# Expert rows gated on the way out and added by the scatter to residual rows in HBM, in a two-layer encoder with a mixture of experts

## The reference

```python
for i in range(2):
    h = rms_norm(x, norm1_g[i])
    x = x + (conformer_conv(h) if i == 0 else diff_attention(h))
    h = rms_norm(x, norm2_g[i])
    x = x + hierarchical_moe(h)

def hierarchical_moe(h):                 # 512 tokens, 32 experts in 4 groups of 8
    grp_p, grp_idx = top_k(softmax(h @ w_grp + b_grp), 1)
    top_p, top_j = top_k(softmax(logits of that group), 2)
    gates = grp_p * top_p / sum(top_p)
    y_e = (silu(x_e @ w1[e]) * (x_e @ w3[e])) @ w2[e]    # rows of the tokens that chose e
    out[token] += gate * y                               # two experts per token
```

## Time and profile before

| | us |
|---|---|
| median of 3 runs | 1585.29 |
| the profiled execution | 1585.1 |
| its span in the profile | 1583.3 |
| TensorE (PE) busy | 1334.0 (84%) |
| VectorE (DVE) busy | 443.3 (28%) |
| ScalarE (ACT) busy | 323.7 (20%) |
| GpSimd (POOL) busy | 268.2 (17%) |
| DMA: 473.40 MB | mean 299 GB/s |
| chain that ended last | PE 46%, DMA 41%, DVE 6% |

### The profile page before, as it was taken

The page is one execution under the profiler, slowest core; times in us unless marked ns, Lnnn a source line. Parts: engine busy times, 40 slices in busy tenths (PEclk is TensorE's granted clock), DMA queues, the critical chain, the costliest instruction groups (busy, mean ns, idle before and its releaser), DMA issues.

```text
span 1583.3 us, 20571 instructions
## 1 busy us (share of the span) xinstructions
PE 1334.0 (84%) x8048; PEld 770.9 (49%) x8048; DVE 443.3 (28%) x957; ACT 323.7 (20%) x638; POOL 268.2 (17%) x370
## 2 busy tenths in 40 slices
PE   7998898998777777774899999999999777777873
PEld 3443456665444444442556666556565444344441
DVE  2898444111010101012344544436111010101002
ACT  3564231000000000001344444322000000000000
POOL 3887000211111111100000000000111111111100
PEclk9999899999999999997899999999999999999997
DMA  8513128999999999996700401436999999999995
GB/s 293 171 44 160 53 93 339 423 420 423 424 425 424 425 424 424 424 422 265 262 1 1 160 1 46 167 127 254 422 421 424 424 424 425 424 425 424 422 414 215
DMA packets 73202, 473.40 MB, mean 299 GB/s; under 512 B 16198, under 2 KB 20294, under 8 KB 38840
## 3 DMA queue, kind: packets, MB, share of 16 engines
q1 hardware_dynamic: 60760, 443.67, 68.2%
q0 software_dynamic: 10080, 16.35, 2.8%
q10 hardware_dynamic: 2304, 12.58, 2.0%
HBM read 465.93 MB, written 23.33 MB: 309 GB/s over the span
## 4 chain that ended last, share of the span: by engine, by line
PE 46%; DMA 41%; DVE 6%; POOL 3%; ACT 2%; issue 1%; SPq 0%; ACTq 0%; POOLq 0%; DVEq 0%
DMA ring<-in_moe_w 36%; PE banks L1454 11%; PE banks L1470 7%; PE banks L1574 6%; PE banks L1603 4%; PE banks L1371 4%; POOL scratch L552 2%; DMA area<-in_moe_w 2%; DVE banks L940 2%; PE banks L1278 2%; PE banks L1357 2%; PE banks L1663 2%; PE banks L1618 1%; PE banks L1298 1%; DMA scratch<-xn_dram,at_in 1%
## 5 line engine op out<-in xcount | busy, mean ns | idle before, releaser
L1454 PE MATMUL banks<-ring,scratch 128*64 128x256 f32 x3776 | 431.5, 382 | 99.4 <-DMA ring<-in_moe_w 96.2
L1454 PEld LDWEIGHTS banks<-ring,scratch 128*64 128x64 f32 x3776 | 285.8, 137 | 263.6 <-DMA ring<-in_moe_w 102.0
L1470 PE MATMUL banks<-ring,scratch 128*64 128x512 f32 x960 | 222.6, 605 | 67.1 <-DMA ring<-in_moe_w 65.0
L1111 DVE COPY scratch<-banks 128x256 f32<-128x256 f32 x65 | 27.6, 424 | 800.8 <-PE banks L1462 800.8
L1470 PEld LDWEIGHTS banks<-ring,scratch 128*64 128x64 f32 x960 | 75.1, 138 | 176.9 <-issue 168.8
L747 ACT ACTIVATE scratch<-banks 128x256 f32<-128x256 f32 x65 | 24.9, 383 | 518.3 <-PE banks L1454 515.1
L1574 PE MATMUL banks<-hT,ring 128*128 128x512 f32 x256 | 120.2, 614 | 0.8 <-DVE hT L894 0.8
L1278 PE MATMUL banks<-hT,ring 128*128 128x512 f32 x256 | 113.1, 602 | 0.8 <-DVE hT L894 0.8
L582 POOL COPY at_out<-rows_out 128x1 int32 (+1 forms) x58 | 10.5, 181 | 594.3 <-ACT scratch L751 594.3
L751 ACT ACTIVATE scratch<-banks 128x512 f32<-128x512 f32 x65 | 38.8, 597 | 344.0 <-PE banks L1470 344.0
L552 POOL TENSOR_TENSOR scratch<-scratch 128x512 f32<-128x512 f32 x77 | 97.9, 1272 | 18.7 <-ACT scratch L714 8.8
(11 more groups left out here) (227 smaller groups left out, 1213.8 us busy)
## 6 DMA issues: line engine op xcount, KB each, us to landing
ring<-in_moe_w SPq DMA_DIRECT2D x178, 2048.0 KB, 27.2
area<-in_moe_w SPq DMA_DIRECT2D x12, 2048.0 KB, 14.7
ring<-in_attn_w_qkv SPq DMA_DIRECT2D x6, 2048.0 KB, 20.3
hT<-in_moe_w SPq DMA_DIRECT2D x5, 2048.0 KB, 17.1
area<-y_dram ACTq DMA_DIRECT2D x8, 1024.0 KB, 7.9
ring<-in_conv_w_in SPq DMA_DIRECT2D x4, 1024.0 KB, 11.2
ring<-in_conv_w_in SPq DMA_DIRECT2D x2, 2048.0 KB, 15.8
ring<-in_conv_w_out SPq DMA_DIRECT2D x2, 2048.0 KB, 23.3
```

Of the source, the lines that this page charges most:

```text
L1454: last = mm(bank[2 + s][q * SLOTS:(q + 1) * SLOTS, k * 256:(k + 1) * 256], xeT[s][:, c % 4, c // 4, :], wc[:, c, q * 256:(q + 1) * 256], s ...
L1470: last = mm(bank[6 + s][q * SLOTS:(q + 1) * SLOTS, :], hidT[s][:, j % 2, j // 2, :], w2c[:, j, q * 512:(q + 1) * 512], start=j == 0, stop= ...
```

## The change

1. **Adding scatter.** For both layers (SUMMED) y_dram holds one row per token, 2 MB; in layer 1 it is the output tensor itself. POOL stores x_res there at the start of a layer's expert stage, 128 tokens at a time, as soon as x_done says that they are final. Each scatter adds its rows to them in the DMA (compute_op ADD), addressed by rows_in, the list the gather uses.
2. **Gate on the way out.** ACT's take_y multiplies by the gate of each slot, gate_rows. That list is made by lists2, in place of rows_out, from the gates split into three bf16 parts (24 matmuls instead of 8), and lists2 now stands between w1 and w3 of turn 1. The gates are therefore worked out earlier. token2 is split into two parts, so lists has 16 matmuls.
3. **A wait.** A scatter may not overlap another one, so each waits for the y_stored of the one before.
4. **End of a layer.** Layer 0 reads 2 MB straight back into x_res; DVE's passes are gone. Layer 1 reads nothing back; SP waits for the last scatters and the kernel ends.
5. **An extra turn.** There are 33 turns. If the last overflowing expert has index 9 or more (EARLY), it changes places with expert 26 (HELD) and its second tile is turn 27, with the units that are still in the ring; one over tile fewer runs then. Otherwise turn 27 runs with empty slots. SP reads the expert for each place from ctl. DVE works out the swap with ten short operations ahead of take_first(l, 0), where two others now stand too, and fills ctl with ten operations after the gates.

The diff, cut to its core:

```diff
-TILES = EXPERTS + OVER
+TURNS = EXPERTS + 1
+TILES = TURNS + OVER
+HELD = 26
+EARLY = 9
+SUMMED = (0, 1)
...
-                with sp.Fori(3, EXPERTS // 2 - 3) as i:
-                    for s in range(2):
-                        loop_units(s, i * 2 + (s + 1))
+                sp.wait_ge(ctl_done, l + 1)
+                def at_place(p):
+                    return sp.value_load(ctl[0:1, bass.ds(p + ORDER, 1)], min_val=0, max_val=EXPERTS - 1)
+                def loop_units(s, p, y_used, up_used):
+                    down_to_ring(3 * s, at_place(p), y, y_used)
+                    e = at_place(p + 2)
+                    to_ring(3 * s + 1, w1_of(e), w1_used, up_used)
+                    to_ring(3 * s + 2, w3_of(e), up, up_used)
...
+                def put_rows(s, done):
+                        g.indirect_dma_start(out=y_dram[l][:, :],
+                                             out_offset=bass.IndirectOffsetOnAxis(ap=at_out[:, s:s + 1], axis=0),
+                                             in_=y_sb[s], in_offset=None,
+                                             bounds_check=y_rows[l] - 1, oob_is_err=False, compute_op=ALU.add).then_inc(done, 16)
...
+                if l in SUMMED:
+                    for t in range(NT):
+                        pool.wait_ge(x_done, X_DONE[l] + t + 1)
+                        g.dma_start(y_dram[l][2 * t * P:2 * (t + 1) * P, :].rearrange("(p h) f -> p (h f)", h=2),
+                                    x_res[:, t, :]).then_inc(x_stored, 16)
...
-                    g.tensor_copy(at_out[:, s:s + 1], rows_out[:, bass.ds(e, 1)]).then_inc(at_copied[l], 1)
+                    g.tensor_copy(at_out[:, s:s + 1], rows_to[:, bass.ds(e, 1)]).then_inc(at_copied[l], 1)
                     pool.wait_ge(at_copied[l], wait_at)
+                    if l in SUMMED and other_stored is not None:
+                        pool.wait_ge(y_stored[l][1 - s], other_stored)
...
-                a.activation(y_sb[s], bank[6 + s][:], ACT.Copy).then_inc(sems["y_taken"], 1)
+                    a.activation(y_sb[s], bank[6 + s][:], ACT.Copy, scale=gate_rows[:, bass.ds(tile, 1)]).then_inc(sems["y_taken"], 1)
...
+                        act.dma_start(x_res[:, t, :], y_dram[l][2 * t * P:2 * (t + 1) * P, :].rearrange("(p h) f -> p (h f)", h=2)
+                                      ).then_inc(y_loaded[t], 16)
...
+                link(v.tensor_scalar(late_cmp, tiles_base, 0.0, None, ALU.is_gt))
+                link(v.tensor_reduce(late, late_cmp, AX.X, ALU.add))
+                link(v.tensor_scalar(late_is, late, float(EARLY), None, ALU.is_ge))
+                link(v.scalar_tensor_tensor(late_d, late, -float(HELD), late_is, ALU.add, ALU.mult))
...
                 take_first(l, 0)
...
+                step(HELD, 0, *up_units(HELD), down_unit(HELD - 1))
+                step(HELD + 1, 1, *up_units(HELD), down_unit(HELD))
+                for p in range(HELD + 1, EXPERTS - 2):
+                    step(p + 1, (p + 1) % 2, *up_units(p), down_unit(p - 1))
```

More of the change, by code:

```diff
@@ L176, in trunk @@
         over_xe = [sem(f"over_xe{l}") for l in range(LAYERS)]
-        over_y = [sem(f"over_y{l}") for l in range(LAYERS)]
+        x_stored = sem("x_stored")
         over_w = [[sem(f"over_w{l}_{k}") for k in range(3)] for l in range(LAYERS)]
@@ new lines, in moe_weights @@
+                with sp.Fori(3, (HELD - 2) // 2) as i:
+                    for s in range(2):
+                        loop_units(s, i * 2 + (s + 1), i * 2 + s, i * 2 + (s + 2))
+                for p in range(HELD - 1, EXPERTS - 4):
+                    loop_units((p - 1) % 2, p, used(p - 2), used(p))
+                e30, e31 = at_place(EXPERTS - 2), at_place(EXPERTS - 1)
+                down_to_ring(MOE_UNITS - 8, at_place(EXPERTS - 4), y, used(EXPERTS - 6))
+                to_ring(MOE_UNITS - 7, w1_of(e30), w1_used, used(EXPERTS - 4))
@@ L491, in _ @@
                         lambda: None)
[L492 to L495, removed]
+            if 1 in SUMMED:
+                for s in range(2):
+                    sp.wait_ge(y_stored[1][s], 16 * (EXPERTS // 2 + 1 - s))
+                sp.wait_ge(moe_over, 2)
+            else:
+                for t in range(NT):
+                    sp.wait_ge(x_done, X_DONE[1] + NT + t + 1)
+                    sp.dma_start(out[0, t * P:(t + 1) * P, :], x_res[:, t, :]).then_inc(out_stored, 16)
+                sp.wait_ge(out_stored, 16 * NT)
         @block.gpsimd
@@ new lines, in route @@
+                n_second = len(second)
+                for b in range(n_second - 1):
+                    link(v.tensor_tensor(hot_part[b], hot_tile, bt(second[b], TILES), ALU.mult))
+                v.tensor_tensor(hot_tile, hot_tile, bt(second[n_second - 1], TILES), ALU.mult).then_inc(hot_done, 1)
+                oc = over_cmp[0:1, :].rearrange("p (j e) -> p j e", e=EXPERTS)
+                first = lambda ap: ap[0:1, :]
+                at = first(late_at)
+                link(v.tensor_scalar(at, first(iota_exp[:]), 99.0, None, ALU.add))
@@ L1098, in take_xT @@
+                dve.wait_ge(lists2_ready, l + 1)
+                if l in SUMMED:
+                    v.tensor_copy(gate_rows[:], bank[6][:, 0:TILES]).then_inc(lists2_done, 1)
+                else:
+                    v.tensor_scalar(rows_out[:], bank[6][:, 0:TILES], far_out[:], None, ALU.add).then_inc(lists2_done, 1)
             def take_xT(l, sems, s, e1):
@@ L1516, in experts @@
                 lists(l)
-                lists2(l)
-                step(1, 1, in_ring(2), in_ring(3), in_ring(4), first=True)
+                step(1, 1, in_ring(2), in_ring(3), in_ring(4), first=True, between=lambda: lists2(l))
                 step(2, 0, in_ring(5), in_extra(0), in_extra(1), first=True)
```

265 lines of the change are left out of this document (162 added, 103 removed).

## The result

The changed kernel takes 1586.35 us, the median of 20 runs (1583.43 to 1588.39). The kernel before took 1583.8 us beside it (20 runs, 1581.24 to 1585.72). The ratio is 1.0017, with a 95% interval of 1.001 to 1.0024. My forecast was 1574.1 us and faster. The time is inside the range that I gave (1561 to 1594), but the sign is wrong: the case within 0.2% had a chance of 0.08.

What follows compares the result with a forecast made beforehand. Weight streaming through the DMA engines was taken to bound the expert stages. Layer 0 (-12.3 - 4.5 + 2.0 + 10 = -4.8) and layer 1 (-18.4 + 2.0 + 10 = -6.4) took 1585.3 to 1574.1 us, range 1561 to 1594.

Steps and rivals of the forecast that it cites:

- the case within 0.2%: Whole kernel: time within about 0.2% (3.2 us) of the kernel before, so no measurable change; chance 0.08.
- What bounds the kernel: Expert stages: DMA streaming of weights sets the pace, TensorE has 4.0 us to spare a turn; added DMA work adds time.
- The add, X = 10: Expert stages: each scattered piece also reads its destination, costing 10 us a layer by byte count, range 4 to 20.
- rival in which the add is dear (X = 20): Expert stages: an adding piece costs three plain ones, 20 us a layer, time 1594 us; chance 0.22.
- the one in which it is nearly free (X under 5): Expert stages: adding costs under 5 us a layer, time 1554 to 1564 us; chance 0.13.
- The extra turn, cost 0: Turn 27, both layers: TensorE 7.6 us late, regains 4.0 us a turn, level after two of five turns; cost 0.
- Routing, 2.0 a layer: Ahead of each expert stage: twelve short DVE operations delay take_first, turn 0 and the weight stream's restart by 2.0 us.
- The new wait: Each scatter waits for the previous one: covered if landings stay under 11 to 15 us; rival of takeover 1652 us, chance 0.04.
- a sign of being wrong: GpSimd (POOL) in mid-stage: waiting for y_stored there would show the forecast wrong; no size given.
- End of layer 0, -12.3 - 4.5: Layer 0's end: over tile gone and last scatter sooner, 12.3 us less; shorter read-back without DVE passes, 4.5 us less.
- End of layer 1, -18.4: Layer 1's end: kernel ends when the last scatter lands, at 1564.9 instead of 1583.3, 18.4 us less.
- That the change doesn't do what it says: Rival: held turn not regained, or layer 0 keeps its over tile; 12 us more, about 1586 us; chance 0.04.

Runs made afterwards that it cites:

- the extra turn alone: Changed kernel with SUMMED = (): no adding scatter in either layer, extra turn and longer routing kept; 1575.81 us, ratio 0.9947 against the kernel before.

## Why the prediction was wrong, point by point

- **What bounds the kernel:** right. Turns of 15.95 us were measured where I had forecast 15.9 to 16.0, and what adds DMA work adds time in proportion.
- **The add, X = 10:** right in size. The stages grew by 10.4 and 10.7 us; against the same kernel without adding it is 10.3 and 13.7 us. The rival in which the add is dear (X = 20) and the one in which it is nearly free (X under 5) both fell.
- **The extra turn, cost 0:** the number was right and its working wrong. The step "2 x 11.6 - 15.6 = 7.6 us late" took only TensorE's work; the order of the stream, w2 of a place behind w1 and w3 of the next one, makes it 16.4. I had it level after two of five turns; it is level after four, and with two turns fewer it costs 13 us.
- **Routing, 2.0 a layer:** wrong, 5.4 and 5.5. The delay of take_first was nearly right (2.5 us). The step that failed is "so is turn 0": I moved turn 0 by the delay and kept its 7.1 us. The gap ahead of it grew from 0.85 to 3.17 us, the granted clock fell, and turn 0 took 10.0. Both layers together are 6.9 us of the 13.0 missed.
- **The new wait:** it doesn't take over. Landings are 10.8 us (median), inside my 9 to 12, and the same waits with ordinary landings cost nothing. In layer 1 GpSimd waits ten times, 31.2 us in all, for the adding scatter before, which I had named as a sign of being wrong. Seven of the ten lie between 1137 and 1222 us, in the early turns of 11.6 us. With half of the scatters adding such waits nearly go (in layer 1 three inside the stage, none over 2.2 us), while the price is still half (459.9 - 453.4 = 6.5 us of 13.7). That speaks for the pieces' own price; a small part from the waits isn't excluded.
- **End of layer 0, -12.3 - 4.5:** the sum is right (-17.3), but by luck, since its parts aren't. The over tile that is gone gives all of it. The gain of the read-back is there with ordinary scatters (27.7 us from the last w2 to the projection, where the extra turn alone has 31.7: 4.0), but the chained landings of adding ones take it back (31.9). From the timeline of GpSimd, the last three issues:

```profile
724.50 1.60 POOL L605 DMA_INDIRECT y_dram<-scratch,at_out  x1 [20.69 <-ACT scratch L811]
...
732.69 1.58 POOL L605 DMA_INDIRECT y_dram<-scratch,at_out  x1 [6.38 <-DMA y_dram<-scratch,at_out]
...
738.11 1.58 POOL L605 DMA_INDIRECT y_dram<-scratch,at_out  x1 [3.64 <-DMA y_dram<-scratch,at_out]
```

- **End of layer 1, -18.4:** wrong, -12.8. The step "now the end is the landing of that scatter, 1561.54 + 2.9 + 0.5" has two faults. The last scatter is issued later behind its last w2 and lands in some 3.7 us, not 2.9 (it is issued at 1577.07): from the end of the last w2 matmuls to the landed scatter it is 6.2 us (1574.63 to 1580.8) instead of the 4.9 of my working (1559.98 to 1564.9). And behind it GpSimd's DRAIN runs until 1584.9, 4.1 us more. It stood in the trace of before, from 1561.7 for 6.8 us, hidden under work that this change removes.
- **That the change doesn't do what it says** had the time (about 1586), but not the cause: the expert was held and the turn regained. That the two agree is chance.

## What to carry to other kernels

When a change shortens the tail of a kernel, look at what every engine still has to do there, the closing DRAIN of GpSimd included: a span ends when the last of them does, and the work that you remove may have covered it. A delay of 2.5 us ahead of TensorE's next burst cost over 5 here, since it opened a gap in which the clock fell; put small serial work behind the step that feeds TensorE. In this kernel an adding piece cost 2.2 ordinary ones: it pays only where what it removes is on the critical path, here in neither layer by more than 2 us. And look at the clock of every stretch before a difference is put down to an edit: 24 matmuls far from any edit differed by 2.5 us.

## What the runs showed of the hardware

- An adding indirect piece of 2 KB (float32) occupies its DMA engine 0.10 us longer than a plain one of some 0.087 us, in proportion to the number of pieces (3.5%, 4.3%, 5.1% of the engines with none, half and all of them adding). It lands later, 10.8 us against 8.0 (median), and GpSimd's issue takes 1.61 us against 1.03.
- GpSimd's closing DRAIN ends 6.1 us behind its last memset or wait, with the last scatter landed (6.12) or under way (1578.76 to 1584.9); behind a plain scatter it was 5.9 us (before).
- Behind 3.17 us without a matmul the granted clock fell to 0.50, and 64 matmuls took 10.0 us instead of 7.13; in other runs, behind the same gap, they took 8.5 to 8.8 or 7.13 us. Behind 0.85 us they took 7.13 in every trace.
- ACT's copy of 128x512 out of PSUM takes 687 ns with a scale for each partition; the one without took 597 in the kernel before. Here that counts only behind a layer's last w2.
